# Seven block products for eight in the second mixer's projections, their factors made one stage earlier

## What is computed

```python
h = _rmsnorm(x, norm_a[i])
x = x + _short_conv_mixer(h, w_in_a[i], conv_a[i], w_out_a[i])     # first mixer; x after it is x1
kv = _rmsnorm(x, norm_kv) @ w_kv                                     # 1024 -> 1024
q, g = jnp.split(_rmsnorm(x, norm_b[j]) @ w_in_b[j], 2, axis=-1)     # 1024 -> 1024
o = _stick_breaking_attention(q, k, v)
x = x + (o * jax.nn.silu(g)) @ w_out_b[j]
...
mod = jnp.einsum('bd,de->be', jax.nn.silu(c), w_ada[l]) + b_ada[l]   # 1024 -> 3072, one row
```

## Time and profile before

| what | before |
|---|---|
| median of 3 runs (lowest, highest) | 3302.05 us (3299.87, 3304.22) |
| the profiled execution, its span | 3304.2 us, 3302.4 us |
| TensorE matmul (PE) busy | 3063.5 us, 93% |
| VectorE (DVE) busy | 2078.1 us, 63% |
| ScalarE (ACT) busy | 1528.6 us, 46% |
| mean granted TensorE clock | 0.969 |
| HBM read, written | 203.92 MB, 108.15 MB |

### The profile page before, as it was taken

How to read it: one execution, slowest core, us unless ns; L and a number is a source line. 1 busy time by engine, 2 the same in 40 slices (tenths; PEclk the granted TensorE clock), 3 DMA queues, 4 the chain that set the end, 5 groups by cost and what they waited for, 6 DMA issues and landing times. The chain is left out here.

```text
span 3302.4 us, 47728 instructions
## 1 busy us (share of the span) xinstructions
PE 3063.5 (93%) x17652; PEld 2414.8 (73%) x17652; DVE 2078.1 (63%) x2990; ACT 1528.6 (46%) x2738; POOL 192.2 (6%) x447
## 2 busy tenths in 40 slices
PE   6999999999899998999998999999877789998799
PEld 5888788888688876677777777776655566776577
DVE  8888877743221217888878456234278888988444
ACT  5443422232111116777779322111277778888400
POOL 0000000000000000110000000000021111112100
PEclk8999999999899998999999999999879999999899
DMA  4443422346543324111135432323631110111665
GB/s 121 120 116 110 140 64 81 113 145 192 197 131 99 115 77 110 34 45 31 43 115 177 127 109 83 127 90 93 165 67 33 29 27 20 24 37 37 144 198 153
DMA packets 350426, 325.06 MB, mean 98 GB/s; under 512 B 72413, under 2 KB 303325, under 8 KB 342897
## 3 DMA queue, kind: packets, MB, share of 16 engines
q1 hardware_dynamic: 344216, 286.06, 30.4%
q0 software_dynamic: 5264, 35.72, 3.0%
q10 hardware_dynamic: 720, 0.31, 0.0%
HBM read 203.92 MB, written 108.15 MB: 94 GB/s over the span
## 5 line engine op out<-in xcount | busy, mean ns | idle before, releaser
L323 ACT ACTIVATE s_mx_w_hi<-s_mx_raw 128x512 fp32r<-128x512 f32 x224 | 139.0, 629 | 319.5 <-PE p_mx_ps L629 154.2
L1347 DVE TENSOR_TENSOR_SCAN s_st_prod<-s_st_soft,s_st_prod 128x512 f32<-128x512 f32 x192 | 234.4, 1267 | 15.8 <-ACT s_st_soft L1276 15.8
L2870 PE MATMUL p_sa_turn<-s_ident,s_sa_arg 128*128 128x128 f32 x1088 | 166.9, 288 | 57.7 <-ACT s_sa_prob L2498 36.2
L1276 ACT ACTIVATE s_st_soft<-p_st_z 128x512 f32<-128x512 f32 (+3 forms) x320 | 153.8, 534 | 111.5 <-PE p_st_z L1397 111.5
L2087 PE MATMUL p_pr_ps<-s_h_hi,s_pr_w_hi 128*128 128x512 f32 (+1 forms) x712 | 195.3, 395 | 10.7 <-ACT s_pr_stage L1934 8.8
L629 PE MATMUL p_mx_ps<-s_h_a_hi,s_mx_w_hi 128*128 128x512 f32 x512 | 199.6, 390 | 1.2 <-issue 1.1
L629 PE MATMUL p_mx_ps<-s_h_a_hi,s_mx_w_lo 128*128 128x512 f32 x512 | 199.2, 389 | 0.0
L629 PE MATMUL p_mx_ps<-s_h_a_lo,s_mx_w_hi 128*128 128x512 f32 x512 | 199.2, 389 | 0.0
L2087 PE MATMUL p_pr_ps<-s_h_lo,s_pr_w_hi 128*128 128x512 f32 (+1 forms) x712 | 193.8, 393 | 0.0
L2087 PE MATMUL p_pr_ps<-s_h_hi,s_pr_w_lo 128*128 128x512 f32 (+1 forms) x712 | 192.7, 391 | 0.0
L2870 PEld LDWEIGHTS p_sa_turn<-s_ident,s_sa_arg 128*128 128x128 f32 x1088 | 119.6, 144 | 99.9 <-issue 63.6
(11 more groups left out here) (365 smaller groups left out, 7454.5 us busy)
## 6 DMA issues: line engine op xcount, KB each, us to landing
s_mx_raw<-in_w_in_a SPq DMA_DIRECT2D x128, 256.0 KB, 3.9
d_kvqg_t<-s_pb_stage SPq DMA_DIRECT2D x16, 1024.0 KB, 5.1
s_pb_ada<-in_w_ada SPq DMA_DIRECT2D x16, 768.0 KB, 6.6
s_pr_raw<-in_w_in SPq DMA_DIRECT2D x21, 512.0 KB, 3.9
s_pr_work<-s_pr_stage SPq DMA_DIRECT2D x38, 256.0 KB, 4.7
d_rot_hi<-s_pr_rot POOLq DMA_DIRECT2D x9, 1024.0 KB, 4.3
d_rot_lo<-s_pr_stage POOLq DMA_DIRECT2D x9, 1024.0 KB, 6.3
d_p_t<-s_pr_stage POOLq DMA_DIRECT2D x9, 1024.0 KB, 8.2
```

The source lines that it names most:

```text
L323: nc.scalar.activation(w_hi[:, m], raw[g % 2][:, m], ACT.Copy).then_inc(hi_done, 1)
L1276: nc.scalar.activation(soft[:, u % DEEP, s, 0:n], z[u % 2 * 2 + s][:, 0:n], ACT.Sigmoid, scale=-SCALE).then_inc(softened, 1)
L1347: nc.vector.tensor_tensor_scan(prod[:, b, s, 0:n][:, ::-1], back, back, carry, ALU.mult, ALU.bypass).then_inc(multiplied, 1)
L2870: ins = nc.tensor.transpose(turn[i % 2][:, c:c + P], arg[:, s % DEEP, side, at + c:at + c + P], ident[:])
```

## The change

The projections are computed as the first mixer's are.

- `phase_project` works in 16 groups of 84 matmuls (8 pairs of weight blocks, for each half of the sequence), 1344 in all. Weights are loaded once for each half (8 MB each). ScalarE multiplies them with the norm's weight (`scale_weights`, 8 of 128x256 a group), VectorE makes 4 sums and 7 low parts, and combines the 7 products by 7 operations of 128x512. Results go out as 128x1024 rows for upper and lower block; for the gate ScalarE applies Silu to them in place.
- `phase_out_a` takes its tiles in pairs, i and i+4 of each half (`ROWS`). From a pair's four transposed blocks ScalarE takes three (`take`), VectorE makes four more by adding (`make`). The factors of the first half stay in SBUF (`RESIDENT`), those of the second go to DRAM (`h_late`) in units of 64 rows (256 bytes each run); the last pair's are made in the next stage. `xo` is gone: the sum is made in place in the buffer of x, so that x of tile n+1 is loaded after x1 of tile n-1 is stored. Three of group 0's products are made here (`begin_next`), and four of its factor pairs split.
- At the end of group 7 the factors of the second half are loaded from `h_late` and split, as in the mixer, each three products before its use (there four).
- `mod` is added up in groups 3 to 6 and 9 to 12 and summed by TensorE in group 13.
- SyncE loads k, q and v of the first heads during the last group (`load_first`); the attention's engines wait for the last stores only before their first writes to `prob` and `o_sb`.
- In the mixer only PSUM names change, and the two tiles that it loads for the next stage are 0 and 4.

The diff, cut to its core:

```diff
@@ phase_mixer @@
-        ps = [next_acc[:].rearrange("p (a n) -> p a n", a=2), *(al.ps(f"mx_ps{n}", [P, 2, PART]) for n in range(1, 4))]
+        ps = [*(of[:].rearrange("p (a n) -> p a n", a=2) for of in acc), *(of[:].rearrange("p a k n -> p a (k n)") for of in pt)]
-                    sp.dma_start(next_y[:, j], y_v[j]).then_inc(next_y_in[j], 16)
+                    sp.dma_start(next_y[:, j], y_v[rows[j]]).then_inc(next_y_in[j], 16)
+                    sp.dma_start(next_x[:, j], x_v[rows[j]]).then_inc(next_x_in[j], 16)
...
@@ new: ProjectSpace and the helpers @@
+    def load_weights(self, sp, weights, g):
+
+        M = Strassen
+        w, p = next((w, p) for w, at in weights for p in [g % 8 - at] if 0 <= p < w.shape[1] // (2 * P))
+        w_v = w.rearrange("(a k p) (b n) -> b a p k n", a=2, p=P, n=P)
+        for slot, block, half in ((M.A11_B11, 0, 0), (M.A21, 1, 0), (M.A12_B21, 0, 1), (M.A22_T4, 1, 1)):
+            sp.dma_start(self.raw[g % 2][:, slot], w_v[2 * p + block, half]).then_inc(self.w_in[g % 2], 16)
...
+    def scale_weights(self, nc, act, g, half):
+
+        M = Strassen
+        act.wait_ge(self.w_in[g % 2], 64 * (g // 2 + 1))
+        act.wait_ge(self.norms_in, 32)
+        first, last = ((M.A11_B11, M.A21), (M.A12_B21, M.A22_T4))[half]
+        for k in range(KH):
+            of = self.raw[g % 2][:, first:last + 1:last - first, k]
+            at = (0 if g % 8 < 4 else KC) + half * KH + k
+            nc.scalar.activation(of, of, ACT.Copy, scale=self.scale[:, at:at + 1]).then_inc(self.scaled, 1)
...
+    def split_hi(self, nc, act, g, m):
+        act.wait_ge(self.summed, 4 * (g + 1))
+        if g:
+            act.wait_ge(self.product, MULTS * (g - 1) + m + 1)
+        nc.scalar.activation(self.w_hi[m][:], self.raw[g % 2][:, m], ACT.Copy).then_inc(self.w_hi_done, 1)
...
+    def x_split_hi(self, nc, act, m):
+        act.wait_ge(self.made, 4 * TILES // 4)
+        nc.scalar.activation(self.x_hi[m][:], self.raw_of(m), ACT.Copy).then_inc(self.x_hi_done, 1)
+
+    def x_split_lo(self, nc, dve, m):
+        dve.wait_ge(self.x_hi_done, m + 1)
+        nc.vector.tensor_tensor(self.x_lo(m), self.raw_of(m), self.x_hi[m][:].bitcast(F32), ALU.subtract).then_inc(self.x_lo_done, 1)
+
+    def multiply(self, nc, bank, m):
+        for k in range(KH):
+            for n, (w, a) in enumerate(split_pass_list(self.w_hi[m][:], self.w_lo[m][:], self.x_hi[m][:], self.x_lo(m))):
+                ins = nc.tensor.matmul(bank, w[:, k, :], a[:, k, :], start=(k == 0 and n == 0), stop=(k == KH - 1 and n == 2))
+        ins.then_inc(self.product, 1)
...
+ROWS = [half * TILES // 2 + i + side * TILES // 4 for half in range(2) for i in range(TILES // 4) for side in range(2)]
...
@@ phase_out_a @@
+            def take(i):
+                act.wait_ge(transposed, 2 * i + 2)
+                blocks = ((M.A11_B11, pt[0][:, 0]), (M.A12_B21, pt[0][:, 1]), (M.S4_B22, pt[1][:, 1]))
+                if i < RESIDENT:
+                    for m, of in blocks:
+                        nc.scalar.activation(proj.raw_of(m)[:, :, i * P:i * P + P], of, ACT.Copy).then_inc(taken, 1)
+                else:
+                    for b in range(2):
+                        if i > RESIDENT:
+                            act.wait_ge(proj.late_out[b], 16 * (i - RESIDENT))
+                        for m, of in blocks:
+                            nc.scalar.activation(proj.whole[b][:, m], of[:, :, b * UNIT:b * UNIT + UNIT], ACT.Copy).then_inc(taken, 1)
+
+            for n in range(TILES):
+                stats(n)
+                if n + DEEP < TILES:
+                    y_split(n + DEEP)
+                if n in (10, 11):
+                    proj.scale_weights(nc, act, 0, n - 10)
+                if n in (12, 13):
+                    proj.x_split_hi(nc, act, n - 12)
+                if n == TILES - 2:
+                    act.wait_ge(y_lo_done, TILES)
+                    for m in range(2):
+                        proj.split_hi(nc, act, 0, m)
+                if n == TILES - 1:
+                    act.wait_ge(product, TILES)
+                    for m in range(2, EARLY + 1):
+                        proj.split_hi(nc, act, 0, m)
+                        proj.x_split_hi(nc, act, m)
+                if n % 2:
+                    take(n // 2)
...
+            def make(i):
+                if i < RESIDENT:
+                    dve.wait_ge(taken, takes(i + 1))
+                    make_factors(nc, dve, lambda m: proj.raw_of(m)[:, :, i * P:i * P + P], made, sums(i), pt[1][:, 0])
+                else:
+                    for b in range(2):
+                        make_unit(nc, dve, proj, pt[1][:, 0], i - RESIDENT, b)
+
+            for n in range(TILES):
+                add(n)
+                norm(n)
+                if n + DEEP < TILES:
+                    y_split(n + DEEP)
+                if n in (12, 13):
+                    for of in range(2):
+                        proj.add_up(nc, dve, 0, 2 * (n - 12) + of)
+                    proj.x_split_lo(nc, dve, n - 12)
+                if n == TILES - 2:
+                    for m in range(2):
+                        proj.split_lo(nc, dve, 0, m)
+                if n % 2 and n < TILES - 1:
+                    make(n // 2)
+            for m in range(2, EARLY + 1):
+                proj.split_lo(nc, dve, 0, m)
+                proj.x_split_lo(nc, dve, m)
...
+            def begin_next(m):
+                pe.wait_ge(proj.w_lo_done, m + 1)
+                pe.wait_ge(proj.x_lo_done, m + 1)
+                pe.wait_ge(added, TILES if m == M.S1_T1 else TILES - 1)
+                proj.multiply(nc, bank_of(banks, 0, m), m)
+
+            for n in range(1, DEEP):
+                multiply(n)
+            for n in range(TILES):
+                transpose(n)
+                if n + DEEP < TILES:
+                    multiply(n + DEEP)
+                if n == TILES - 2:
+                    begin_next(0)
+            for m in range(1, EARLY):
+                begin_next(m)
...
@@ phase_project @@
+    steps_at = {}
+    for e in range(STEPS):
+        steps_at[(3 + e // 2 if e < 8 else 9 + (e - 8) // 2), (2, 5)[e % 2]] = e
+    late_at = {divmod(MULTS * LAST + m + LAG, MULTS): m for m in range(MULTS)}
...
+                if g == LAST:
+                    for m in range(MULTS):
+                        sp.wait_ge(product, MULTS * LAST + m + 1)
+                        sp.dma_start(proj.raw_of(m), h_late[:, m]).then_inc(late_in[m], 16)
...
+            next_space.load_first(sp, out_t, (upper_out, 16 * END), product, MULTS * END)
             sp.wait_ge(mod_out, 32)
+            store(END)
...
+            keep_first(0)
+            for m in range(EARLY + 1, MULTS):
+                proj.split_hi(nc, act, 0, m)
+                proj.x_split_hi(nc, act, m)
+                if m >= MULTS - 2:
+                    proj.scale_weights(nc, act, 1, m - MULTS + 2)
+            for g in range(GROUPS):
+                for m in range(MULTS):
+                    if m == 0 and g:
+                        keep_first(g)
+                        if (g - 1) % EACH >= GATES:
+                            open_lower(g - 1)
+                    if g + 1 < GROUPS:
+                        proj.split_hi(nc, act, g + 1, m)
+                    if (g, m) in late_at:
+                        late_split(late_at[g, m])
+                    if g == 2 and m == MULTS - 2:
+                        act.wait_ge(mod_in, 48)
+                        nc.scalar.activation(c_col, c_col, ACT.Silu).then_inc(c_ready, 1)
+                    if m in (3, 4) and g + 2 < GROUPS:
+                        proj.scale_weights(nc, act, g + 2, m - 3)
+                    if m == MULTS - 1 and g % EACH >= GATES:
+                        open_upper(g)
+            open_lower(END)
...
+            for m in range(EARLY + 1, MULTS):
+                proj.split_lo(nc, dve, 0, m)
+                proj.x_split_lo(nc, dve, m)
+                combine(0, m - EARLY)
+            for g in range(GROUPS):
+                for m in range(MULTS):
+                    if g or m > EARLY:
+                        combine(g, m)
+                    if g == 0 and m == 0:
+                        for n in range(4):
+                            proj.add_up(nc, dve, 1, n)
+                    if g + 1 < GROUPS:
+                        proj.split_lo(nc, dve, g + 1, m)
+                    if g == 0 and m >= MULTS - 2:
+                        make_unit(nc, dve, proj, pt[1][:, 0], PAIRS - 1, m - MULTS + 2)
+                    if (g, m) in late_at:
+                        late_split(late_at[g, m])
+                    if (g, m) in steps_at:
+                        modulate(steps_at[g, m])
+                    if g == SUM_AT and m:
+                        stage_mod(m - 1)
+                    if m >= MULTS - 2 and g + 2 < GROUPS:
+                        for n in range(2):
+                            proj.add_up(nc, dve, g + 2, 2 * (m - MULTS + 2) + n)
...
```

(22 more changed lines are left out.)

661 lines of the change are left out of this document (346 added, 315 removed).

## The result

The changed kernel took 3247.91 us, median of 4 runs (3247.18 to 3256.07), against 3301.46 for the kernel before in the same runs: ratio 0.9843, 95% interval 0.9825 to 0.986. The profiled execution took 3248.2 us, its span 3246.2. The forecast was 3243, its range 3231 to 3259. So the total came out as predicted, but two of its terms did not, and the stages behind, which the sum took as unchanged, hid most of the difference.

A forecast was written before the change was run, and what follows sets the result against it. TensorE alone was taken to bound the changed stages. From the end of tile 14's transposes to the attention, 27.0 + 285.7 + 8.0 + 5.2 + 7.1 = 333.0 us against 392.4; 59.4 less than 3302.05 gives 3243 us, range 3231 to 3259.

The forecast's parts named there:

- Number and length of steps: Projections: 1344 matmuls for 1536, each 0.2267 us by staying in one bank; 304.7 us, a gain of 54.9.
- the step stays: Projections: step tied to columns and operands, not banks, so 0.234 us; 9.8 us more, 3253; chance 0.07.
- First seam: Output projection to projections: group 1 starts 27.0 us after W, tile 14's transposes; seam 8.0 for 15.9, gain 7.9.
- Groups: Projections, groups 1 to 15: 19.05 us each, the work of VectorE and ScalarE all hidden behind TensorE.
- Change of factors: Projections, groups 7 and 8: VectorE has 26.2 us of work against 19.0; cost 8.0, low end 5.4, high end 13.
- transfers starve the change: Groups 7 and 8: some 11 MB in 30 us exceeds the measured DMA rate; 3250 to 3256 us; chance 0.15.
- Sum of mod: Projections, group 13: 12 matmuls moved from the end to where nothing hides them; 5.2 us more there.
- Second seam: Last projection product to the attention's first product: 7.1 us for 16.9, gain 9.8, bounds 6 and 11.
- Output projection: Stage before the projections: added VectorE work costed at nothing, its chain about 9 of the 10.9 us a `multiply` covers.
- The stages behind: From the attention's first product on: they only start earlier, costed at no change.

The follow-up runs named there:

- e1: Kernel before, loop over the four row chunks moved outermost in the 1344 block-product matmuls; these took 312.3 us, the whole 3306.4 (before 3308.4, one run each).
- e12: Kernel before, loops untouched, 96 bytes of padding ahead of the high part of h and 160 behind; 3292.61 us, 0.997 of before.
- e10: Changed kernel with SyncE's list reordered, late factors split four products ahead and group 9's preparation moved behind them; change of factors 4.6 us, 3238.5 us in one run.
- e4: Changed kernel without VectorE's low parts of the late factors, products reading the high parts instead; change of factors 6.6 us, whole 3471 us on other data.
- e8: Changed kernel, mod summed by 24 matmuls with mod as stationary operand, all behind group 13's first product; group 13 took 30.06 us, the sum 11.0 for 7.6.
- e9: Kernel before, e1's loop order plus 32 bytes of padding ahead of and behind the high part of h; 1344 matmuls 310.9 us, 3303.6 in all.
- e2: Changed kernel, loads of the first two late factors ahead of group 9's weights and both stores, mod's load behind all seven; change of factors 14.2 us.

## Why the prediction was right in the sum and wrong in two terms

- **Number and length of steps: right in size, wrong in reason.** 1344 steps of 0.2267, and group after group of 19.04. But I read the 3% between L1014 and L1020 as the bank's. e1 and e12 show that in the kernel before it is the tiles' places. The rival "the step stays" had named "columns and operands" and had the bank right; that the step was short all the same is luck, since the changed kernel's tiles happen to lie alike. Of the 54.9 us foreseen, the 192 matmuls left out are the algorithm's; some 9 are the tiles' placement. The Trainium skill ("TensorE: Matmul & The Clock Gate", Back-to-back issue gap) makes the isolated gap depend on the columns alone, 216 ns for 512. The runs agree with it against my reason, as the order and the bank moved the step by under 0.4% (e1), but not in full: at equal columns it differed by 3%, 0.2267 to 0.234, and even the shorter is 5% above the page's figure.
- **First seam: right**, 26.7 for 27.0, though TensorE waited once for 2.4 us and once for 1.5, not "2 to 3 us twice"; 0.6 more is the edge between the stages.
- **Groups: right but for 1.3 us.** "All of it is hidden, by the same margin as in the mixer" counted VectorE's work (96.5 us in 134.6) and not its wait for the store of the upper results. At group 2 that wait (2.9 us) reached TensorE. The scaling of 128x256 is recorded with 0.50 and steps 0.40 in a row, near the 0.42 taken.
- **Change of factors: the step that failed.** "26.2 against 19.0, so 7.2 us are too much ... I take 8.0". The work was counted rightly. Left out were three waits: the first factor is issued 7.4 us after its place is free and lands at 1017.6; VectorE stands idle for 6.0 us just ahead of the stretch, for a store behind the same two blocked entries of SyncE's list; and ScalarE and VectorE wait for each other over the next weights. The high end, 13, was passed. The rival "transfers starve the change" was right in part: the sign set for it, a hole ended by a transfer, is there at product 0, DMA moved 366 GB/s from 1005 to 1035, and its price, 7 us more, is near the 6.7 by which the 8.0 fell short. But its cause, the rate, falls with e10; it was the place in the list. I had counted what is queued on SyncE behind each wait for the weights, not for this stretch.
- **Sum of mod: mis-sized**, 7.6 for 5.2; I moved a block that ran in a row and priced it in a row, while the change spreads it over six places, each with its own 0.2 us, and slower first steps behind.
- **Second seam: right**, 7.4 for 7.1. **Output projection: right**, no hole but the stage's first, 0.3 us idle and the same before; 176.5 of 176.84 busy.
- **The stages behind: taken as unchanged.** They took 2041.3 us from the attention's first product to the last matmul, 8.7 less, and hid most of the 10.3. That the result lies within 3238 to 3250 is luck by these 8.7 us; the stated range would have held without them (3248.2 + 8.7 = 3256.9). Over the eight profiles of the changed kernel and its variants (e4, with its other data, aside) this stretch was 2041.3 to 2048.7, over the five of the kernel before and its variants 2046.4 to 2052.7, and the profile of before stood at 2050.0. So a part is scatter between executions and some 5 us may be systematic, mostly in the selecting attention (733 to 736 us against 735 to 741). VectorE's busy time there is the same, the granted clock 0.94 against 0.93. The clock does not order the profiles, though: e8 had 0.925 and 734.4 us in this stage, e9 0.934 and 738.9. What ties it to the change was not found, and no run was made for it.

## What to carry to other kernels

Work that fits an engine's time can still bind if the engine, in order, stands in front of a wait just before its crowded stretch: list, for each transfer that such a stretch needs or waits for, what stands ahead of it in the queue and what that waits for, and take preparation that is not due yet out of the stretch on every engine at once. Moving one entry alone can bring nothing where several waits end together (e2). When two loops differ in the step of equal matmuls, compare the places of their tiles before their order. And a total that comes out as predicted proves none of its terms.
